# Prompt attention in twos of steps: scores, transposes and values regrouped on TensorE, banks opened by the first product, output copies moved

## The reference

```python
for w, d in DILATED_GROUPS:            # (128,1), (512,4), (2048,16)
    ...
    s = jnp.einsum('brnqhc,brnkhc->brnhqk', qg, kb, preferred_element_type=jnp.float32) * scale
    ...
    s = jnp.where(mask[None], s, NEG_INF)
    m = jnp.max(s, axis=-1, keepdims=True)
    p = jnp.exp(s - m)
    den = jnp.sum(p, axis=-1)
    ...
    o = jnp.einsum('brnhqk,brnkhc->brnqhc', p, vb.astype(jnp.float32)) / den_t[..., None]
...
out = jnp.sum(alpha[..., None] * o_all, axis=0) / jnp.sum(alpha, axis=0)[..., None]
```

## Time and profile before

| | |
|---|---|
| time, 3 runs | 1903.97 us median, 1903.89 to 1905.54 |
| the profiled execution's own time | 1905.57 us |
| its span, first to last instruction | 1903.8 us |
| TensorE busy (matmul) | 1862.9 us, 98% |
| VectorE, ScalarE, GpSimd busy | 64%, 37%, 35% |
| mean granted TensorE clock | 0.996 |
| attention of the prompt on TensorE | 741.8 to 865.6 us of the span |

### The profile page before, as it was taken

How to read it: one execution, slowest core, us unless ns; L and a number is a source line. 1 busy time by engine, 2 the same in 40 slices (tenths; PEclk the granted TensorE clock), 3 DMA queues, 4 the chain that set the end, 5 groups by cost and what they waited for, 6 DMA issues and landing times.

```text
span 1903.8 us, 35890 instructions
## 1 busy us (share of the span) xinstructions
PE 1862.9 (98%) x15190; PEld 1774.0 (93%) x15190; DVE 1211.2 (64%) x1512; ACT 708.7 (37%) x944; POOL 660.3 (35%) x338
## 2 busy tenths in 40 slices
PE   8999999999999999999999999999999999999997
PEld 8999999989889898778999999899999999999996
DVE  8899652255444645673445736885555575878988
ACT  6311221244434445663200134423444445333332
POOL 0122111211111113443466641136777761432504
PEclk9999999999999999999999999999999999999998
DMA  5422533866776744732354332533334466655333
GB/s 176 116 90 80 137 112 104 260 186 206 224 221 210 234 154 135 198 115 102 125 180 151 130 119 77 172 129 105 144 125 163 162 211 244 211 188 191 125 126 138
DMA packets 191416, 298.73 MB, mean 157 GB/s; under 512 B 37249, under 2 KB 133249, under 8 KB 187681
## 3 DMA queue, kind: packets, MB, share of 16 engines
q1 hardware_dynamic: 184352, 270.60, 44.5%
q10 hardware_dynamic: 6912, 25.96, 3.4%
HBM read 215.12 MB, written 79.28 MB: 155 GB/s over the span
## 4 chain that ended last, share of the span: by engine, by line
PE 83%; DVE 8%; DMA 4%; issue 2%; ACT 2%; POOL 1%; SPq 0%; POOLq 0%; DVEq 0%; ACTq 0%
PE ps L2644 37%; PE ps L3175 25%; PE ps L3019 3%; PE ps L2983 2%; PE ps L3109 2%; PE ps L2903 1%; PE ps L2816 1%; PE ps L3095 1%; PE ps L2659 1%; PE ps L2797 1%; PE ps L2873 1%; PE ps L2912 1%; DMA w_raw<-in_w 1%; PE ps L2778 1%; PE ps L2764 1%
## 5 line engine op out<-in xcount | busy, mean ns | idle before, releaser
L1161 POOL TENSOR_TENSOR w_lo<-w_raw,w_hi 128x1024 fp32r<-128x1024 f32 x48 | 121.5, 2532 | 623.4 <-ACT w_hi L1310 623.4
L2644 PE MATMUL ps<-op_hi,w_hi 128*128 128x352 f32 x1392 | 309.0, 330 | 0.1
L2644 PE MATMUL ps<-op_lo,w_hi 128*128 128x352 f32 x1392 | 301.8, 325 | 0.0
L2644 PE MATMUL ps<-op_hi,w_lo 128*128 128x352 f32 x1392 | 300.2, 323 | 0.0
L2644 PEld LDWEIGHTS ps<-op_hi,w_hi 128*128 128x128 f32 x1392 | 233.5, 188 | 15.2 <-issue 13.2
L2644 PEld LDWEIGHTS ps<-op_lo,w_hi 128*128 128x128 f32 x1392 | 237.5, 188 | 0.0
L2644 PEld LDWEIGHTS ps<-op_hi,w_lo 128*128 128x128 f32 x1392 | 236.8, 188 | 0.0
L1384 ACT ACTIVATE stage<-ps 128x1056 f32<-128x1056 f32 x48 | 50.5, 1053 | 280.7 <-PE ps L2644 280.7
L1168 POOL TENSOR_TENSOR w_hi<-w_raw,zeros 128x1024 fp32r<-128x1024 f32 x24 | 59.3, 2470 | 173.4 <-PE ps L3109 63.0
L3175 PE MATMUL ps<-do_hi,w_hi 128*128 128x264 f32 x560 | 114.0, 285 | 2.5 <-DVE w_lo L2470 1.0
L3175 PE MATMUL ps<-do_lo,w_hi 128*128 128x264 f32 x560 | 113.2, 284 | 0.0
(11 more groups left out here) (477 smaller groups left out, 4613.5 us busy)
## 6 DMA issues: line engine op xcount, KB each, us to landing
w_raw<-in_w SPq DMA_DIRECT2D x101, 512.0 KB, 4.1
t_raw<-tmp_h SPq DMA_DIRECT2D x28, 1056.0 KB, 5.5
kc<-in_k_cache SPq DMA_DIRECT2D x48, 448.0 KB, 5.3
vc<-in_v_cache SPq DMA_DIRECT2D x48, 448.0 KB, 6.0
out_keep<-stage ACTq DMA_DIRECT2D x24, 528.0 KB, 2.7
tmp_gate_d<-stage ACTq DMA_DIRECT2D x24, 528.0 KB, 5.2
gate_t<-tmp_gate_d SPq DMA_DIRECT2D x24, 528.0 KB, 3.7
tmp_h<-o_t SPq DMA_DIRECT2D x18, 528.0 KB, 3.1
```

What stands on the lines that cost most here:

```text
L1161: pool.tensor_tensor(lo, w_raw[:, b], hi.bitcast(F32), ALU.subtract).then_inc(w_split[b], 1)
L2644: mm = pe.matmul(ps[:, 3 * dst + q, 0:BLK], w[:, b, w0 + n], x[:, k, q * BLK:(q + 1) * BLK], start=(n == 0 and part == 0), stop=(n == len( ...
```

## The change

TensorE's queue goes by twos of steps. For even g: scores(g + 4), v of a pair if due, scores(g + 5), transposes(g), near values of g - 2 and g - 1 with the far ones behind both, transposes(g + 1). The signal at_pv now counts these visits, so that waits for it name `visits(g) = g // 2 + 1`. V_STEPS puts the v of pairs 2 and 4 one step later than before (behind g = 9 and 23; the others behind 1, 15, 29). The copies to pt wait for the last values that read the same part (LAST_USE), no longer for the whole pair before. The product of zeros is gone: the first product into a bank opens it. near_block goes by query blocks: a value tile that served two query blocks in one product of 256 columns now serves each in a product of 128. The output copies on VectorE come in the odd step behind the visit that completes their bank. GpSimd's queue, the maxima, the exponentials, and what each product computes are as before.

```diff
-V_STEP = 1
+V_STEPS = [PER * _w + 1 + _w % 2 for _w in range(HP - 1)]
...
+LAST_USE = [3, 3, 3, 3, 5, 5, 6]
...
+def visits(g):
+
+    return g // 2 + 1
...
-                wait(dve, at_pv, g - g % PER - 1)
+                if g >= PER:
+                    dve.wait_ge(at_pv, visits(g - g % PER - PER + LAST_USE[g % PER]))
...
-                if g % PER == 4:
-                    at_outputs(g // PER, 7)
-                if g % PER == 0 and g:
-                    at_outputs(g // PER - 1, 6)
+                for w in range(HP):
+                    if g == 2 * visits(PER * w + 3) + 1:
+                        at_outputs(w, 7)
+                    if g == 2 * visits(PER * w + PER - 1) + 1:
+                        at_outputs(w, 6)
...
-            def near_block(w, j, uses):
-
-                q, n = uses[0][0], len(uses)
+            def near_block(w, j, q, b, opens=False, closes=False):
+
                 for a, rows in enumerate(heads):
-                    at_block = [8 * max(x - 1, 0) + 4 * a + b for x, b in uses]
-                    got = pt_blocks[:, at_block[0]:at_block[-1] + 1:at_block[-1] - at_block[0] if n > 1 else 1]
-                    mm = pe.matmul(ps[rows, 6 + q // 4, P * (q % 4):P * (q % 4 + n)].rearrange("p (q n) -> p q n", q=n),
-                                   vn[:, w % 2, j, rows], got, start=False, stop=(j == 1))
+                    mm = pe.matmul(ps[rows, 6 + q // 4, P * (q % 4):P * (q % 4 + 1)], vn[:, w % 2, j, rows],
+                                   pt_blocks[:, 8 * max(q - 1, 0) + 4 * a + b], start=opens, stop=closes)
                 return mm
...
-                if s in (0, 4):
-                    pe.matmul(ps[:, 7 - s // 4, :], zeros[:, 0:P].bitcast(F32R), zeros[:].bitcast(F32R), start=True, stop=False)
-                for j in STEP_TILES[s]:
-                    uses = [(j, 2 if j == 1 else j > 0)]
-                    if j % 4 != 3:
-                        uses.append((j + 1, int(j == 0)))
-                    if j == 4:
-                        near_block(w, 3, [(4, 0)])
-                    mm = near_block(w, j, uses)
+                    wait(te, at_o, 2 * w - 1 + (s == 4))
+                for q in STEP_TILES[s]:
+                    mm = near_block(w, q, q, 2 if q == 1 else q > 0, opens=q in (7, 3))
+                    if q:
+                        mm = near_block(w, q - 1, q, int(q == 1), closes=q == 1 and w % 2 == 0)
                 return mm
...
-            def at_outputs(g):
-                mm = at_near(g)
-                if g % PER in (3, 5):
-                    mm = at_far(g)
+            def at_outputs(first):
+                for g in (first, first + 1):
+                    mm = at_near(g)
+                for g in (first, first + 1):
+                    if g % PER in (3, 5):
+                        mm = at_far(g)
                 mm.then_inc(at_pv, 1)
...
-            for g in range(NG + 1):
+            for g in range(0, NG, 2):
                 if g + AHEAD < NG:
                     at_scores(g + AHEAD)
-                if g < NG:
-                    at_transposes(g)
+                if g - 1 in V_STEPS:
+                    at_values((g - 1) // PER + 1)
+                if g + AHEAD < NG:
+                    at_scores(g + AHEAD + 1)
+                at_transposes(g)
                 if g:
-                    at_outputs(g - 1)
-                if g % PER == V_STEP and g // PER + 1 < HP:
-                    at_values(g // PER + 1)
+                    at_outputs(g - 2)
+                at_transposes(g + 1)
+            at_outputs(NG - 2)
```

More of the change, by code:

```diff
@@ L161 @@
     GRAN += 2
-    if _g % PER == V_STEP and _g // PER + 1 < HP:
+    if _g in V_STEPS:
         V_GRAN[_g // PER + 1] = [GRAN, GRAN + 1]
         GRAN += 2
+LAST_USE = [3, 3, 3, 3, 5, 5, 6]
+def visits(g):
+    return g // 2 + 1
 def members(g):
@@ L812, in far_values @@
                 if w >= 2:
-                    sy.wait_ge(at_pv, PER * (w - 1))
+                    sy.wait_ge(at_pv, visits(PER * (w - 1) - 1))
                 past(sy, far_v, 48 * w)
@@ L1479, in at_copy @@
                 act.wait_ge(at_t, P_GRAN[g][0] + 1)
-                wait(act, at_pv, g - g % PER - 1)
+                if g >= PER:
+                    act.wait_ge(at_pv, visits(g - g % PER - PER + LAST_USE[g % PER]))
                 s.activation(pt[:, q - 1, 0, 0:n].rearrange("p j m -> p (j m)"), ps[:, 4, 0:n * P], ACT.Copy).then_inc(at_even, 1)
@@ L1486, in at_values @@
                 if w >= 2:
-                    act.wait_ge(at_pv, PER * (w - 1))
+                    act.wait_ge(at_pv, visits(PER * (w - 1) - 1))
                 s.activation(vn[:, w % 2, 0:4].rearrange("p j m -> p (j m)"), ps[:, 4, :], ACT.Copy).then_inc(at_even, 1)
@@ L1504, in _ @@
                 at_copy(g)
-                if g % PER == V_STEP and g // PER + 1 < HP:
+                if g in V_STEPS:
                     at_values(g // PER + 1)
@@ L2169, in at_values @@
                 if w >= 2:
-                    dve.wait_ge(at_pv, PER * (w - 1))
+                    dve.wait_ge(at_pv, visits(PER * (w - 1) - 1))
                 v.tensor_copy(vn[:, w % 2, 4:8].rearrange("p j m -> p (j m)"), ps[:, 5, :]).then_inc(at_odd, 1)
             def at_outputs(w, bank):
-                dve.wait_ge(at_pv, PER * w + (4 if bank == 7 else PER))
+                dve.wait_ge(at_pv, visits(PER * w + (3 if bank == 7 else PER - 1)))
                 wait(dve, yo_out[w % 2], 16 * (w // 2))
@@ L2920, in at_near @@
                 if g == 0:
-                    te.wait_ge(w_zero, 1)
                     te.wait_ge(sa_o, ROUNDS)
-                if w and s in (0, 4):
-                    te.wait_ge(at_o, 2 * w - 1 + (s == 4))
                 if s in (0, 4):
-                    pe.matmul(ps[:, 7 - s // 4, :], zeros[:, 0:P].bitcast(F32R), zeros[:].bitcast(F32R), start=True, stop=False)
-                for j in STEP_TILES[s]:
-                    uses = [(j, 2 if j == 1 else j > 0)]
-                    if j % 4 != 3:
-                        uses.append((j + 1, int(j == 0)))
-                    if j == 4:
-                        near_block(w, 3, [(4, 0)])
-                    mm = near_block(w, j, uses)
+                    wait(te, at_o, 2 * w - 1 + (s == 4))
[3 more added lines that the diff above has]
+                        mm = near_block(w, q - 1, q, int(q == 1), closes=q == 1 and w % 2 == 0)
                 return mm
@@ L2946, in at_far @@
                                            start=False,
-                                           stop=(c == 1 and x == RES - 1))
+                                           stop=((c == 1 if s == 3 else w % 2 == 1) and x == RES - 1))
                 return mm
-            def at_outputs(g):
-                mm = at_near(g)
-                if g % PER in (3, 5):
-                    mm = at_far(g)
+            def at_outputs(first):
[4 more added lines that the diff above has]
+                        mm = at_far(g)
                 mm.then_inc(at_pv, 1)
```

## The result

The changed kernel takes 1910.95 us (median of 7 runs, 1907.86 to 1913.74) against 1903.97; the ratio is 1.0032, with a 95% interval of 1.0022 to 1.0043, so 4.2 to 8.2 us slower. A second set of runs gave 1911.03 and 1.0029 (1.0019 to 1.0038). The forecast was 1905.6, at most 1909.8. The profiled execution took 1910.95, its span is 1909.1, and the attention on TensorE, from the first scores to the first GLU product, takes 130.23 us (742.40 to 872.63) where it took 123.81 (741.79 to 865.60).

What follows compares the result with a forecast made beforehand. TensorE's queue was taken as the bound. Zeros -2.8, shape changes -6.1, far_k waits +9.0, pair 2's load -0.7, start +1.2, late transposes +0.5, tail +0.6 sum to +1.7 us: 1903.97 becomes 1905.6, range 1903.5 to 1908, with rivals 1899.8 to 1909.8.

Steps and rivals of the forecast that it cites:

- The bound: TensorE's queue sets the time unless something makes it wait; its matmul side is busy 98% of the span.
- the zeros: On TensorE, 12 products of zeros at 0.23 us each, two per pair, go away: -2.8 us.
- the split: Near values on TensorE, 72 products of 256 columns become 144 of 128: taken as 0, at most +0.7 us.
- the wait on far_k and its chain: TensorE's first scores of the next pair wait five times for GpSimd's gather, 4.75 us after transposes(7w + 1): +9.0 us.
- The transposes that VectorE makes late: TensorE's transposes wait some 0.2 us for VectorE's copy in four rounds and a little in others: +0.5 us.
- the tail: At the end, VectorE's output copy of bank 7 stands between the low parts TensorE waits for: +0.6 us.
- the idle stretches of the first round: At the start, scores(5) wait for maxima(3) and first transposes come later: +0.2 to +1.7, taken as +1.2 us.
- scores behind scores: Adjacent score groups on TensorE, nineteen in the loop, might still leave over a shape change: bounds 0 and +2.0, taken as nothing.
- the 0.16: Price in us of a change of array shape on TensorE; 38 fewer changes give -6.1 us.
- the second rival: On TensorE, shape changes stay or split products cost: 1909.7 us at most, 1908 in the middle; chance 0.16 with the fourth.
- that rival: VectorE becomes late for the transposes through bunched scores and output copies: +6.6, 1912 us without any slack; chance 0.09.
- the load of pair 3: SyncE's load has 4 us to spare: 0, and up to 2 us once if that goes.

Runs made afterwards that it cites:

- experiment 2: The changed kernel with SyncE's load of pair w + 2 issued ahead of the values' round trip of pair w + 1: 1911.10 us, ratio 1.0037.
- experiment 1: The changed kernel with GpSimd gathering the next pair's far_k ahead of the normalization of step s = 4: 1905.51 us, ratio 1.0004.
- experiment 3: The changed kernel with both far_k gathered early and the load of pair w + 2 issued early: 1902.17 us, ratio 0.9990.
- 9: The changed kernel with far_k and load early, and TensorE's first round back in the old order: 1900.31 us, ratio 0.9981.
- experiment 10: The changed kernel with only TensorE's first round back in the old order: 1907.38 us, ratio 1.0018.
- 7: The kernel before with all but the regrouping: no zeros, near values by query blocks, far_k and load early: 1903.36 us, ratio 0.9989.
- experiment 8: The changed kernel with VectorE's output copies back in their old places, steps s = 4 and s = 0: 1935.78 us, ratio 1.0160.
- experiment 5: The changed kernel run again with nothing altered: 1911.03 us, ratio 1.0029.
- experiment 6: The changed kernel with SyncE's load of pair w + 2 ahead of the values' round trip, run once more: 1911.65 us, ratio 1.0037.

## Why the prediction was right and where it was wrong

**Right.** The bound, the size of the zeros (0.44 in a pair against 0.47), the split at nothing, the wait on far_k and its chain (4.75 forecast, 4.68 to 4.71 measured; five waits of 9.0 together forecast, 8.5 measured in experiment 2; experiment 1 took them away). The sign and the main story, that what TensorE sheds is eaten by that wait, hold. The transposes that VectorE makes late (0.2 forecast, 0.29 measured) and the tail (+0.6 forecast; from the first GLU product to the last wait's end 6.35 before and 6.83 after, +0.5) came as said.

**The steps that failed** are two terms of the sum: one that was left out, and one that was taken as nothing. The terms of the wait are not among them: by the table's means the changed kernel lost 6.5 us where the sum gives 1.7, 4.8 more, and with the waits gone (experiment 3) it gained 1.7 where the sum without +9.0 gives 7.3, so 5.6 are missing there too.

**Left out: the clock.** The sum was made as if the granted clock stayed as it was in the earlier trace rows. The table has 7.5 us before and 10.2 after, +2.7 (± 1.0), and about 2 of it goes with the idle stretches of the first round (9 and 10). The prediction saw those (+0.2 to +1.7) and priced them as idle time only.

**Taken as nothing: scores behind scores.** "I take nothing" stood on values behind values. Measured, these neighbours shed 0.15, 0.05 and 0 of the 0.16, so a pair is 0.3 us longer: 20.47 for 20.2. Between the five waits on far_k lie four pairs, +1.1; the upper bound given (+2.0) held it. Where nothing waits more of it shows: of the 1.9 us that two pairs should shed, 0.8 to 1.1 were shed (7). With both terms, 1.7 + 2.7 + 1.1 = 5.5, and 6.5 was measured.

**The range** ended at 1909.8 by the second rival, scores behind scores and splits; the true sum needed the clock on top. VectorE was late by no more than the forecast's own term; experiment 8 shows how near that rival lay.

**The loads.** The prediction gave the load of pair 3 4 us to spare and didn't name that of pair 5. Pair 3's is late by 0.8 us in one profile of the changed kernel (5) and by 1.5 in experiment 10, pair 5's by 2.2 and 1.0 in the two profiles of the changed kernel. In the medians this costs nothing measurable (2 and 6), since far_k's chain is as long; only behind an early far_k it counts (3.3 us between 1 and 3). My theory on reading the result, that load and low clock at 840 are the missing 4 us, fell with the second experiment. Here too the step that failed was to take one execution's picture for the kernel's.

What stays open: 1.0 us of the sum, which is within the noise of the terms; the load may be part of it (the wait at 839 cost 1.1 more than far_k's own in the first profile, nothing in the second). Open too is which idle pattern makes the clock fall in one execution and not in the next.

## What to carry to other kernels

Work shed from the fullest engine counts only up to the shortest distance between two of its instructions that a chain through other engines joins. Look for signals that come just in time before the change (here 0.22 us), measure the chain from its head on the full engine, and move its last link up in the same step. When visits are grouped, go through every wait on other engines' queues that names a visit: output copies that stood too early for the visits they wait for cost 25 us in all. And where a change leaves the full engine idle for a microsecond at a time, add the clock to the sum, from the mean granted clock of many executions and not from the one that was profiled.

## What the runs showed of the hardware

How far the granted clock lies below full speed is a property of a kernel only in the mean: 7.5 us by the table for the kernel before over 86 executions, 22.8 for experiment 8, with falls at 744, 776, 816, 840 or 1104 to 1136 in single profiles. Nearly every profile also has one or two gaps of 0.4 to 1.9 us in the attention on TensorE, put down to "issue", often inside a group of one kind, as in the earlier trace rows: 1.28 there, 1.93 at 816 in experiment 5, 1.61 at 808 in experiment 6, none of that size behind 751 in the first profile of the changed kernel. They come back at the same instructions with another length: experiments 2 and 6, one kernel, have 1.06 and 1.61 before the same far values, and 0.55 and 0.82 before the same scores. They add to the spread, and nothing in the profile explains them. And a group of scores in array tiles of 64*32 that follows another one doesn't save the whole 0.16 us of a change of shape, while values in 128*64 do (1.02 for 512 columns in either form).
